# Small DMAs on the sync engine's queue, four gemm banks for two more units, and three reorderings in a two-block fp32 kernel

## Chip, cores and metric

One core of a Trainium2 chip (8 cores; the others are unused). The metric is the device time of one execution of the whole program in microseconds, as the median of several runs.

## What is computed

A token matrix x (512 tokens, width 1024, fp32) goes through two blocks. The first block, cut to what matters:

```python
h = rmsnorm(x, norm1_g); u = h @ w_in
y_a = short_conv_mixer(u_a); y_b = stick_breaking_attention(q_b, k_b, v_b)
y_c = mamba2_mixer(u_c);     y_d = moba_attention(q_d, k_d, v_d)      # 4 heads of 64 each
merged = sum(sigmoid(u_g[i]) * (y[i] @ w_branch[i]))                  # 4 branches
x = x + merged @ w_o
g, up = split(rmsnorm(x, norm2_g) @ w_gate_up)                        # hidden width 2816
x = rmsnorm(x + (silu(g) * up) @ w_down, final_g)
```

The second block takes that x. Its attention has 16 query heads and 2 key/value heads of 64, a window of three chunks of 64 keys for each chunk of 64 queries, a sink logit for each head, and a rotation of the first 16 of 64 features:

```python
h = rmsnorm(x, norm_g); q, k, v, za, u, vs, zs, gm = split(h @ w_in2)
q, k = partial_rope(q), partial_rope(k)
a  = (window_sink_attention(q, k, v, sinks) * silu(za)) @ w_att_out
sg = (chunked_spatial_gating(gelu(u), gelu(vs)) * silu(zs)) @ w_sg_out
ga, gs = split(sigmoid(gm + b_merge))
out = rmsnorm(x + (ga * a + gs * sg) @ w_o2, final_g_2)
```

## The kernel before

**Products.** Every large product is fp32 made of three passes in fp32r: a weight is split into a high part `whi` (rounded by ACT, `split`, L947) and a low part `wlo` (the difference, GpSimd, `rest`, L446), an activation into `hh` and `hl` in the same way, and TensorE sums hi*hi, lo*hi and hi*lo (`gemm_fm`, L497: L519, L520, L527). Activations lie feature-major: a tile is 128 features by 512 tokens, one PSUM bank. Weights come in units of 1024 x 256 (`raw`, `whi` and `wlo` have two slots each); a unit gives two tiles, in the branch stage four. Tile numbers T run through the whole program (`tiles_before`, L321). TensorE counts a finished tile in `tile_done`, DVE counts an evicted one in `tile_free`; before tile T TensorE waits for `free_before(T)` evictions.

**Order of the units.** Units 0 to 11 are the projections of the first block, 12 to 27 the gates and branches, 28 to 31 w_o, 32 to 65 the feed-forward in three parts (the last part ends with a down projection of 6 products in depth), 66 the second block's keys and values (tiles 164, 165), 67 to 74 its queries and za in turn (q0, za0, q1, za1, ...; tiles 166 to 181), 75 to 78 vs, then gates with w_att_out, u with zs, gates with w_sg_out, and w_o2. The bank of a tile is T mod 4, except from unit 67 (`n_qz`) to the first gate unit, where it is T mod 2, because banks 2 and 3 (`gemm23`) then hold the attention's odd steps:

```python
def bank_of(T):                                            # L325
    return G[T % 2] if tiles_before(n_qz) <= T < tiles_before(n_ga + 1) else G[T % 4]
def free_before(T):                                        # L329
    return T - 1 if tiles_before(n_qz) <= T < tiles_before(n_ga + 2) else T - 3
```

**SP (L345)** issues every load in order. It waits for the unit's slot (`slot_free`, L356: GpSimd has made the low part of the unit before last), then issues. `stream` (L372) and `stream_pairs` (L415) do that in hardware loops, L383 and L424.

**Small steps between the tiles.** The first block's heads are handled in steps that a table puts behind tiles (`MIX`, L471, `run_mix`): slot 24 + 2i + j is after tile j of branch unit 12 + i. moba's scores (`mo1`, L643) for heads 0 to 3 are in slots 25, 27, 29, 31, stick-breaking's (`st1`, L685) in 34, 37, 40, 43. TensorE works in two row halves there: `array_halves` (L292) takes one half of the rows from q and k and the other from `qs`, `ks`, copies with the two 64-partition halves exchanged. These copies are four DMAs of 256 KB, issued by ACT in slots 24 and 33 (`st_swap`, L1081 to L1091), in order with ACT's other work.

**Residual and norm.** In the w_o stage (DVE L1667, ACT L1141) and in the last down projection (DVE L1708, ACT L1167) each tile m goes round: DVE adds the residual into xT (L1665); ACT makes one (`sq0`) or two squares (`sq1`, `sq2`, L1174, L1175) and then rounds hh (L1150, L1176); DVE forms hl (L1670, L1711) and adds the squares into sums (`accumulate`, L1661). The first tile of the next unit needs hh and hl of all eight m. From the sums ACT and DVE then make the norm's factors, R with them (L1724).

**Into the second block.** DVE evicts the keys (L1734 to L1740: `rope_s` and four 64-row pieces of `k2`), then the values (`wpt`, L1742), scales all of xT by the final gain and factor (L1744 to L1746, eight operations), reads the transposed factors (L1748) and the transposed gating weights (L1751), and adds the rotated part to the keys (`finish_keys`, L1760). The rotation wants `rope_s` with rows 0 to 7 and 8 to 15 of each half exchanged, in `rope_t`; ACT issues these copies (`swap_halves`, L1232): eight for the keys, four for each pair of query tiles. DVE adds `rope_t` to a query pair (L1840) just before it evicts the za tile behind it.

**Attention.** 32 steps s, four for each tile m of two heads. Each engine has a `w_slot` that handles several steps at once, in this order:

```python
# TensorE, L859             # ACT, L1220              # DVE, L1806
w_values(i - 4)             w_out(i - 4)              w_soft(i);  w_norm(i - 1)
w_turn(i - 3)               w_turned(i - 3)           w_rest(i - 5)
w_scores(i)                 w_exp(i)                  w_out(i - 4)
```

TensorE's `w_scores(s)` (L816) waits for `w_p`, the normalised weights of step s - 2, whose bank it takes. `w_turn` transposes the weights, ACT's `w_turned` (L1203) copies them to `wpt`, `w_values` (L846) multiplies by v. Every fourth step DVE's `w_out` (L1794) makes `att_t` and ACT's `w_out` (L1214) rounds it. TensorE's slots stand in the middle and between its gemm tiles (`hook`), from tile 170 on.

Of the kernel before, what the change touches and what calls it, by code (L numbers as in the profile page):

```python
# [28 lines left out]
P = 128  # L29
# [46 lines left out]
def build_program(nc, x, par, cst1, cst2a, w_in, w_branch, w_o, w_gu, w_down, w_in2, sg_w, sg_b, ln_g,  # L76
# [8 lines left out]
    with ctx:  # L85
# [239 lines left out]
        def bank_of(T):  # L325

            return G[T % 2] if tiles_before(n_qz) <= T < tiles_before(n_ga + 1) else G[T % 4]

        def free_before(T):  # L329

            return T - 1 if tiles_before(n_qz) <= T < tiles_before(n_ga + 2) else T - 3
# [13 lines left out]
        def _(sp):  # L345
# [46 lines left out]
            for q, br in enumerate(ORDER):  # L392
                stream(n_b0 + 4 * q, 4, both(tiles_of(w_in, IN_G + br * DM), tiles_of(w_branch[br], 0, 0, 2, raw_b)))
# [32 lines left out]
            stream_pairs(n_qz, (w_in2, I2_Q), (w_in2, I2_ZA))  # L426
            stream(n_vs, 4, both(tiles_of(w_in2, I2_VS)))
# [54 lines left out]

        for st, at in enumerate((24, 33)):
            MIX.setdefault(at, []).append(("swap", st))
# [9 lines left out]
        def _(pe):  # L494
# [219 lines left out]
            def st_st3(h):  # L714
                pe.wait_ge(sem("st_w"), h + 1)
                if h >= 1:
# [5 lines left out]
                      "st3": st_st3, "swap": lambda st: None}  # L722
# [93 lines left out]
            def w_scores(s):  # L816
# [3 lines left out]
                if s == 0:  # L820
                    pe.wait_ge(sem("k_ready"), 1)
                if s >= 2:
                    pe.wait_ge(sem("w_p"), s - 1)
# [35 lines left out]
            def w_slot(limit):  # L859
                i = pos[0]  # L860
                if i >= limit and limit < STEPS:
                    return
                if 0 <= i - 4 < STEPS:
# [3 lines left out]
                if i < STEPS:  # L867
                    w_scores(i)
# [75 lines left out]
        def _(act):  # L944
# [136 lines left out]
            def st_swap(st):  # L1081

                if st == 0:
                    act.wait_ge(sem("yc_lo"), 2)
                    act.wait_ge(sem("tile_free"), tiles_before(8))
                else:
                    act.wait_ge(sem("mo_s"), HEADS)
                    act.wait_ge(sem("tile_free"), tiles_before(11))
                for half, whole in ((qs, (qd, qb)[st]), (ks, (kd, kb)[st])):
                    for to in (0, 64):  # L1090
                        act.dma_start(half[to:to + 64, :, :], whole[64 - to:P - to, :, :]).then_inc(sem("swapped"), 16)  # L1091

            none = lambda *a: None
            stages = {"dt": none, "dtT": st_dtT, "xsT": none, "acs": none, "cb": st_cb, "mh1": st_mh1, "mh2": none, "mn": st_mn,
                      "mo1": st_mo1, "mo2": st_mo2, "mo3": st_mo3, "st1": st_st1, "st2": st_st2, "st3": st_st3, "swap": st_swap}
# [45 lines left out]
            for p in range(4):  # L1141
                for j in range(2):
# [857 lines left out]
```

## Time and profile before

| | us |
|---|---|
| three runs | 1403.67, 1404.04, 1406.64 (median 1404.04) |
| the profiled execution's own time | 1403.01 |
| its span, first to last instruction | 1401.2 |
| TensorE busy | 1356.1 (97%) |
| DVE, GpSimd, ACT busy | 614.2, 593.1, 512.1 |
| mean granted TensorE clock | 0.991 |

The page's table of slices shows TensorE busy in nine tenths or more of nearly every slice; the exceptions are the first slice and two at 840 to 880 us, where the granted clock is lower too. Engines wait in queues of their own, so idle time of an engine other than TensorE says little by itself. The DMA engines are busy 30% of the time.

### The profile page before, as it was taken

The numbers are of one execution on the slowest core, as the hardware profiler recorded it, in microseconds if no ns is written. First come the engines' busy times: TensorE is split into PE (matmuls) and PEld (weight loads), VectorE is DVE, ScalarE is ACT, GpSimd is POOL, SyncE is SP. The second block draws the span as 40 slices with busy tenths as digits, with TensorE's granted clock in tenths as the row PEclk, the third lists the DMA queues.
The fourth block names the chain that finished last, engine by engine and source line by source line (L and its number), as shares of the span: only waits on it lengthen the run. The fifth ranks groups of instructions, "written<-read, shape, count | busy, mean of one in ns | idle before, by whom it ended". The sixth has DMA issues, their size and how long they took to land.

```text
span 1401.2 us, 17740 instructions
## 1 busy us (share of the span) xinstructions
PE 1356.1 (97%) x6782; PEld 1104.8 (79%) x6782; DVE 614.2 (44%) x1043; ACT 512.1 (37%) x741; POOL 593.1 (42%) x448
## 2 busy tenths in 40 slices
PE   7999999999999999999999996999999999999997
PEld 5888877788888888888888875777778888888885
DVE  3575444465544343223412356466564432333343
ACT  5222444545433443122212244244454322533232
POOL 4453333333454365444445542433322444535441
PEclk9999999999999999999999997999999999999999
DMA  6231342313224342233333223222211222232221
GB/s 197 72 109 61 90 128 76 105 38 113 76 68 151 90 120 90 90 91 107 102 90 90 75 75 108 65 94 66 64 61 61 89 91 91 74 107 90 90 91 60
DMA packets 144560, 126.41 MB, mean 90 GB/s; under 512 B 4272, under 2 KB 142640, under 8 KB 144496
## 3 DMA queue, kind: packets, MB, share of 16 engines
q1 hardware_dynamic: 143472, 122.77, 28.5%
q10 hardware_dynamic: 1024, 2.75, 0.9%
q8 instruction: 45, 0.74, 0.2%
q14 instruction: 19, 0.16, 0.0%
HBM read 120.66 MB, written 2.10 MB: 88 GB/s over the span
## 4 chain that ended last, share of the span: by engine, by line
issue 43%; POOL 28%; PE 26%; DVE 1%; ACT 1%; POOLq 0%; DVEq 0%; ACTq 0%
POOL wlo L455 27%; PE gemm L519 7%; PE gemm L520 7%; PE gemm L527 7%; PE gemm L541 1%; PE gemm L542 1%; PE gemm L543 1%; POOL wlo_b L451 1%; PE mix L854 1%; PE mix L842 1%; PE mix L911 1%; DVE sml L1876 0%; DVE wp L1790 0%; PE gemm L831 0%; PE mix L831 0%
## 5 line engine op out<-in xcount | busy, mean ns | idle before, releaser
L455 POOL TENSOR_TENSOR wlo<-raw,whi 128x512 fp32r<-128x512 f32 x428 | 572.9, 1371 | 625.6 <-ACT whi L959 625.6
L519 PE MATMUL gemm<-hh,whi 128*128 128x512 f32 x1168 | 466.6, 400 | 13.5 <-DVE hl L1711 4.8
L520 PE MATMUL gemm<-hl,whi 128*128 128x512 f32 x1168 | 458.7, 393 | 0.0
L527 PE MATMUL gemm<-hh,wlo 128*128 128x512 f32 x1168 | 290.4, 391 | 0.0
L959 ACT ACTIVATE whi<-raw 128x2048 fp32r<-128x2048 f32 x107 | 204.3, 1910 | 217.6 <-PE gemm L527 188.2
L519 PEld LDWEIGHTS gemm<-hh,whi 128*128 128x128 f32 x1168 | 221.6, 190 | 71.3 <-issue 11.5
L520 PEld LDWEIGHTS gemm<-hl,whi 128*128 128x128 f32 x1168 | 221.8, 190 | 45.1 <-issue 0.7
L527 PEld LDWEIGHTS gemm<-hh,wlo 128*128 128x128 f32 x1168 | 220.4, 189 | 46.5
L451 POOL TENSOR_TENSOR wlo_b<-raw_b,whi_b 128x512 fp32r<-128x512 f32 x16 | 20.7, 1293 | 156.1 <-ACT whi L959 156.1
L519 PE MATMUL gemm<-ah,whi 128*128 128x512 f32 x176 | 68.8, 391 | 3.2 <-DVE al L1693 3.2
L520 PE MATMUL gemm<-al,whi 128*128 128x512 f32 x176 | 68.5, 389 | 0.0
L1686 DVE TENSOR_TENSOR fu_t<-gemm,R 128x512 f32<-128x512 f32 x22 | 15.2, 692 | 102.9 <-PE gemm L527 102.9
L541 PE MATMUL gemm<-whi,hh 128*128 128x256 f32 x192 | 56.6, 295 | 0.6 <-POOL wlo L455 0.6
L542 PE MATMUL gemm<-whi,hl 128*128 128x256 f32 x192 | 54.2, 282 | 0.0
L543 PE MATMUL gemm<-wlo,hh 128*128 128x256 f32 x192 | 54.2, 282 | 0.0
L1633 DVE TENSOR_TENSOR gt<-gemm,R 128x512 f32<-128x512 f32 x32 | 22.0, 689 | 59.0 <-PE gemm L527 58.9
L976 ACT ACTIVATE gt<-gt 128x512 f32<-128x512 f32 x32 | 20.2, 631 | 73.4 <-DVE gt L1633 73.4
L1161 ACT ACTIVATE fg_t<-fg_t 128x512 f32<-128x512 f32 x22 | 13.9, 633 | 83.2 <-DVE fg_t L1684 83.2
L527 PE MATMUL gemm<-ah,wlo 128*128 128x512 f32 x176 | 43.9, 390 | 0.0
L1705 DVE TENSOR_TENSOR xT<-xT,gemm 128x512 f32 x16 | 11.0, 688 | 72.1 <-PE gemm L527 72.1
L519 PEld LDWEIGHTS gemm<-ah,whi 128*128 128x128 f32 x176 | 33.0, 188 | 11.2 <-DVE al L1693 4.5
L541 PEld LDWEIGHTS gemm<-whi,hh 128*128 128x128 f32 x192 | 36.6, 191 | 5.1 <-issue 5.0
(364 smaller groups left out, 1837.0 us busy)
## 6 DMA issues: line engine op xcount, KB each, us to landing
raw<-w_in SPq DMA_DIRECT2D x56, 1024.0 KB, 5.3
raw<-w_gu SPq DMA_DIRECT2D x44, 512.0 KB, 4.8
raw<-w_o SPq DMA_DIRECT2D x8, 1024.0 KB, 5.2
raw<-w_down SPq DMA_DIRECT2D x16, 512.0 KB, 4.0
raw_b<-w_branch SPq DMA_DIRECT2D x16, 256.0 KB, 5.6
raw<-w_ao SPq DMA_DIRECT2D x4, 1024.0 KB, 5.1
raw<-w_so SPq DMA_DIRECT2D x4, 1024.0 KB, 5.2
raw<-w_down SPq DMA_DIRECT2D x8, 384.0 KB, 3.3
```

The lines of the kernel that those rows point to most:

```text
L451: nc.gpsimd.tensor_tensor(a(wlo_b), a(raw_b), as_f32(a(whi_b)), ALU.subtract)
L455: last = nc.gpsimd.tensor_tensor(a(wlo), a(raw), as_f32(a(whi)), ALU.subtract)
L519: mm(bank[:, :], w, xh[:, k, :], start=(k == 0), stop=False)
L520: mm(bank[:, :], w, xl[:, k, :], start=False, stop=False)
L527: last = mm(bank[:, :], wlo_[:, s, k, col:col + P], xh[:, k, :], start=False, stop=(k == kts - 1))
L541: mm(o, hh[:, k, tok], whi[:, s, k, w], start=(k == 0), stop=False)
L542: mm(o, hl[:, k, tok], whi[:, s, k, w], start=False, stop=False)
L543: last = mm(o, hh[:, k, tok], wlo[:, s, k, w], start=False, stop=(k == KD - 1))
L959: fn(a(whi), a(raw), ACT.Copy).then_inc(sem("hi_done"), 1)
L976: return fn(dst, src, ACT.Tanh, scale=scale)
L1633: tt(g, G[T % 4][:, :], R[:, :], ALU.mult).then_inc(sem("tile_free"), 1)
L1686: tt(fu_t[:, s, :], G[(T + 1) % 4][:, :], R[:, :], ALU.mult).then_inc(sem("tile_free"), 1)
```

## The change

Four `dma_start` groups move from ACT's stream to SP's; two limits in `bank_of` and `free_before` move from unit 67 to unit 69, with one more wait on TensorE; the order inside the attention slot changes on TensorE and ACT; eight xT scalings of DVE move from before the factor read to the za tiles; ACT rounds before it squares in two stages. SP's loops for the first eight branch units, for the q/za pairs and for vs are written out.

```diff
         def bank_of(T):
-            return G[T % 2] if tiles_before(n_qz) <= T < tiles_before(n_ga + 1) else G[T % 4]
+            return G[T % 2] if tiles_before(n_qz + 2) <= T < tiles_before(n_ga + 1) else G[T % 4]
         def free_before(T):
-            return T - 1 if tiles_before(n_qz) <= T < tiles_before(n_ga + 2) else T - 3
+            return T - 1 if tiles_before(n_qz + 2) <= T < tiles_before(n_ga + 2) else T - 3
# SP
-            for q, br in enumerate(ORDER):
+            def swap_rows(q, k):
+                for half, whole in ((qs, q), (ks, k)):
+                    for to in (0, 64):
+                        sp.dma_start(half[to:to + 64, :, :], whole[64 - to:P - to, :, :]).then_inc(sem("swapped"), 16)
+
+            for q, br in enumerate(ORDER[:2]):
+                for u in range(4):
+                    n = n_b0 + 4 * q + u
+                    slot_free(n)
+                    load(n, cols(w_in, IN_G + br * DM + u * UC, UC))
+                    load(n, cols(w_branch[br], u * UC, UC, 0, 2), raw_b[:, n % 2])
+                    if n == n_b0 + 1:
+                        sp.wait_ge(sem("yc_lo"), 2)
+                        sp.wait_ge(sem("tile_free"), tiles_before(8))
+                        swap_rows(qd, kd)
+                    if n == n_b0 + 5:
+                        sp.wait_ge(sem("mo_s"), HEADS)
+                        sp.wait_ge(sem("tile_free"), tiles_before(11))
+                        swap_rows(qb, kb)
+            for q, br in enumerate(ORDER[2:], 2):
                 stream(n_b0 + 4 * q, 4, both(tiles_of(w_in, IN_G + br * DM), tiles_of(w_branch[br], 0, 0, 2, raw_b)))
...
-            stream_pairs(n_qz, (w_in2, I2_Q), (w_in2, I2_ZA))
-            stream(n_vs, 4, both(tiles_of(w_in2, I2_VS)))
+            def swap_rotary(p):
+                sp.wait_ge(sem("tile_free"), tiles_before(n_qz + 2 * p) + 2)
+                for r in (0, 64):
+                    for a, b in ((0, 8), (8, 0)):
+                        sp.dma_start(rope_t[r + a:r + a + 8, :, :], rope_s[r + b:r + b + 8, :, :]).then_inc(sem("rope_in"), 16)
+            for p in range(4):
+                for j, c0 in enumerate((I2_Q, I2_ZA)):
+                    n = n_qz + 2 * p + j
+                    slot_free(n)
+                    load(n, cols(w_in2, c0 + p * UC, UC))
+                    if p == 0 and j == 1:
+                        sp.wait_ge(sem("tile_free"), tiles_before(n_e0) + 1)
+                        for r in (0, 64):
+                            for a, b in ((0, 8), (8, 0)):
+                                for kv in range(2):
+                                    sp.dma_start(rope_t[r + a:r + a + 8, kv, :], rope_s[64 * kv + b:64 * kv + b + 8, 0, :])\
+                                        .then_inc(sem("rope_in"), 16)
+                    if p >= 1 and j == 0:
+                        sp.wait_ge(sem("k_ready"), 1)
+                        swap_rotary(p - 1)
+            slot_free(n_vs)
+            load(n_vs, cols(w_in2, I2_VS, UC))
+            swap_rotary(3)
+            for u in range(1, 4):
+                slot_free(n_vs + u)
+                load(n_vs + u, cols(w_in2, I2_VS + u * UC, UC))
# TensorE, w_scores
                 if s == 0:
                     pe.wait_ge(sem("k_ready"), 1)
+                if s == 1:
+                    pe.wait_ge(sem("tile_free"), tiles_before(n_qz + 2))
# TensorE, w_slot
+                if i < STEPS:
+                    w_scores(i)
                 if 0 <= i - 4 < STEPS:
                     w_values(i - 4)
                 if 0 <= i - 3 < STEPS:
                     w_turn(i - 3)
-                if i < STEPS:
-                    w_scores(i)
# ACT, w_o stage, and in the same way in the last down projection (hh ahead of sq1, sq2)
+                    fn(hh[:, m, :], xT[:, m, :], ACT.Copy, scale=pcol("g2", m)).then_inc(sem("h2_hi"), 1)
                     fn(sq0[:, m % 2, :], xT[:, m, :], ACT.Square).then_inc(sem("sq0"), 1)
-                    fn(hh[:, m, :], xT[:, m, :], ACT.Copy, scale=pcol("g2", m)).then_inc(sem("h2_hi"), 1)
# ACT, w_slot (st_swap and swap_halves are removed with their calls)
-                if 0 <= i - 4 < STEPS:
-                    w_out(i - 4)
                 if 0 <= i - 3 < STEPS:
                     w_turned(i - 3)
                 if i < STEPS:
                     w_exp(i)
+                if 0 <= i - 4 < STEPS:
+                    w_out(i - 4)
# DVE, before the factor read
-            for m in range(KD):
-                last = stt(out=xT[:, m, :], in0=xT[:, m, :], scalar=pcol("fg", m), in1=r1[:, :], op0=ALU.mult, op1=ALU.mult)
-            link(last)
# DVE, behind each q and za tile
+                        if u == 1:
+                            stt(out=xT[:, m, :], in0=xT[:, m, :], scalar=pcol("fg", m), in1=r1[:, :], op0=ALU.mult, op1=ALU.mult)\
+                                .then_inc(sem("x_scaled"), 1)
+            dve.wait_ge(sem("x_scaled"), KD)
```

## Rows read from the trace of the kernel before

**Rows 1.** The page, busy time of the engines.
```profile
PE 1356.1 (97%) x6782; PEld 1104.8 (79%) x6782; DVE 614.2 (44%) x1043; ACT 512.1 (37%) x741; POOL 593.1 (42%) x448
```

**Rows 2.** Who waited for whom, TensorE: us in total, times, longest us.
```profile
PE mix L854 <- ACT wpt L1209: 6.1, 6, 1.1
PE gemm L519 <- DVE hl L1711: 4.8, 1, 4.8
PE gemm L519 <- DVE k L1738: 3.8, 1, 3.8
...
PE mix L695 <- DMA ks<-kb: 2.3, 1, 2.3
```

**Rows 3.** Windows, three stretches behind TensorE's waits; PEclk is the granted clock.
```profile
core 0: us, PE busy (x) PEld busy (x) DVE busy (x) ACT busy (x) POOL busy (x), PEclk, DMA share, GB/s
...
267.50:272.10 4.60, 4.57 (x15) 3.28 (x16) 0.00 (x0) 2.74 (x6) 3.37 (x3) 0.63 0.05 6
...
854.70:860.50 5.80, 5.76 (x14) 4.12 (x15) 2.10 (x3) 2.29 (x2) 4.72 (x4) 0.61 0.04 11
...
870.40:876.20 5.80, 5.80 (x14) 4.54 (x15) 5.80 (x9) 0.00 (x0) 0.00 (x0) 0.50 0.09 17
```

**Rows 4.** Timeline, around the second half-swap: start us, us, engine, line, operation [idle before].
```profile
241.37 0.59 PE L654 MATMUL mix<-kd,qd 64*128 64x256 f32 x2
...
256.43 0.37 SPq L383 DMA_DIRECT2D raw<-w_in  x1
...
259.45 2.17 ACTq L1091 DMA_DIRECT2D ks<-kb  x2
...
267.53 0.66 PE L695 MATMUL mix<-qb,kb 64*128 64x512 f32 x1 [2.30 <-DMA ks<-kb]
```

**Rows 5.** Timeline, the last down projection: DVE, then ACT, then GpSimd.
```profile
814.22 0.69 DVE L1665 TENSOR_TENSOR xT<-xT,gemm 128x512 f32<-128x512 f32 x1 [2.21 <-PE gemm L527]
...
818.31 0.69 DVE L1665 TENSOR_TENSOR xT<-xT,gemm 128x512 f32<-128x512 f32 x1
...
844.85 0.68 DVE L1665 TENSOR_TENSOR xT<-xT,gemm 128x512 f32<-128x512 f32 x1
847.45 1.67 DVE L1711 SCALAR_TENSOR_TENSOR hl<-xT,sml,hh 128x512 fp32r<-128x512 f32 x1 [1.93 <-ACT hh L1176]
849.05 2.37 DVE L1661 TENSOR_TENSOR acc<-acc,sq 128x512 f32<-128x512 f32 x2
...
853.93 0.75 DVE L1711 SCALAR_TENSOR_TENSOR hl<-xT,sml,hh 128x512 fp32r<-128x512 f32 x1 [1.92 <-ACT hh L1176]
...
846.71 0.71 ACT L1176 ACTIVATE hh<-xT,sml 128x512 fp32r<-128x512 f32 x1
...
844.82 5.45 POOL L455 TENSOR_TENSOR wlo<-raw,whi 128x512 fp32r<-128x512 f32 x4 [5.51 <-ACT whi L959]
```

**Rows 6.** Timeline from tile 165 to tile 170; last, the page's median to landing.
```profile
860.52 0.79 PE L519 MATMUL gemm<-hh,whi 128*128 128x512 f32 x1
...
867.55 2.79 DVE L1738 SCALAR_TENSOR_TENSOR k<-gemm,cs 64x512 f32<-64x512 f32 x4
...
870.37 5.90 ACTq L1241 DMA_DIRECT2D rope_t<-rope_s  x8
...
888.25 0.50 PE L519 MATMUL gemm<-hh,whi 128*128 128x512 f32 x1 [2.11 <-DVE rope_q L1847]
...
893.80 1.23 DVE L1840 TENSOR_TENSOR q<-rope_q,rope_t 128x1024 f32<-128x1024 f32 x1 [4.41 <-DMA rope_t<-rope_s]
...
899.27 0.39 PE L519 MATMUL gemm<-hh,whi 128*128 128x512 f32 x1
...
raw<-w_in SPq DMA_DIRECT2D x56, 1024.0 KB, 5.3
```

**Rows 7.** Timeline of one attention slot (TensorE, DVE, ACT); last, DVE's waits for odd scores.
```profile
1028.13 0.44 PE L854 MATMUL mix<-wpt,v 128*64 128x128 f32 x4 [0.98 <-ACT wpt L1209]
...
1025.23 1.12 DVE L1790 TENSOR_TENSOR wp<-mix,sml 64x384 f32<-64x384 f32 x2
...
1027.12 0.63 ACT L1218 ACTIVATE ath<-att_t 128x512 fp32r<-128x512 f32 x1 [5.35 <-DVE att_t L1798]
...
DVE gemm L1777 <- PE gemm L831: 24.7, 13, 2.5
```

More of the change, by code:

```diff
@@ L481, in build_program @@
                         MIX.setdefault(at, []).append(step)
-        for st, at in enumerate((24, 33)):
-            MIX.setdefault(at, []).append(("swap", st))
         def run_mix(stages, slot):
@@ L721, in _ @@
                       "mn": st_mn, "mo1": st_mo1, "mo2": st_mo2, "mo3": st_mo3, "st1": st_st1, "st2": st_st2,
-                      "st3": st_st3, "swap": lambda st: None}
+                      "st3": st_st3}
             for n in range(N_A):
@@ L1079, in st_st3 @@
                 out_hi(M[3], "st_o", yh[0], "yb_hi", h)
[L1081 to L1091, printed above, removed]
             none = lambda *a: None
             stages = {"dt": none, "dtT": st_dtT, "xsT": none, "acs": none, "cb": st_cb, "mh1": st_mh1, "mh2": none, "mn": st_mn,
-                      "mo1": st_mo1, "mo2": st_mo2, "mo3": st_mo3, "st1": st_st1, "st2": st_st2, "st3": st_st3, "swap": st_swap}
+                      "mo1": st_mo1, "mo2": st_mo2, "mo3": st_mo3, "st1": st_st1, "st2": st_st2, "st3": st_st3}
             def st_mh2(h):
@@ L1173, in _ @@
                         act.wait_ge(sem("acc2"), m - 1)
+                    fn(hh[:, m, :], xT[:, m, :], ACT.Copy, scale=fgng[:, m:m + 1]).then_inc(sem("h3_hi"), 1)
                     fn(sq1[:, m % 2, :], xT[:, m, :], ACT.Square)
                     fn(sq2[:, m % 2, :], xT[:, m, :], ACT.Square, scale=pcol("fg", m)).then_inc(sem("sq12"), 1)
-                    fn(hh[:, m, :], xT[:, m, :], ACT.Copy, scale=fgng[:, m:m + 1]).then_inc(sem("h3_hi"), 1)
             split(n_e0 + 1)
@@ L1229, in w_slot @@
                     w_exp(i)
+                if 0 <= i - 4 < STEPS:
+                    w_out(i - 4)
                 pos[0] += 1
-            def swap_halves(tiles, T):
-                act.wait_ge(sem("tile_free"), T)
-                for r in (0, 64):
-                    for a, b in ((0, 8), (8, 0)):
-                        if tiles == 2:
-                            act.dma_start(rope_t[r + a:r + a + 8, :, :], rope_s[r + b:r + b + 8, :, :]).then_inc(sem("rope_in"), 16)
-                        else:
-                            for kv in range(2):
-                                act.dma_start(rope_t[r + a:r + a + 8, kv, :], rope_s[64 * kv + b:64 * kv + b + 8, 0, :])\
-                                    .then_inc(sem("rope_in"), 16)
             def attention_gate(m):
@@ L1249, in attention_gate @@
                 sigmoid(za_e[:, m % 2, :], za_tile(m)).then_inc(sem("za_e"), 1)
-            swap_halves(1, tiles_before(n_e0) + 1)
             for p in range(4):
@@ L1256, in _ @@
                     for j in range(2):
-                        if u == 1 and j == 0:
-                            swap_halves(2, tiles_before(n) + 2)
                         w_slot(lim)
@@ L1588, in _ @@
             stages = {"dt": st_dt, "dtT": st_dtT, "xsT": st_xsT, "acs": st_acs, "cb": st_cb, "mh1": st_mh1, "mh2": st_mh2, "mn": st_mn,
-                      "mo1": st_mo1, "mo2": none, "mo3": st_mo3, "st1": st_st1, "st2": st_st2, "st3": st_st3, "swap": none}
+                      "mo1": st_mo1, "mo2": none, "mo3": st_mo3, "st1": st_st1, "st2": st_st2, "st3": st_st3}
             for n in range(N_A):
```

## The prediction

> **What bounds the kernel now.** TensorE does: the page gives it 1356.1 us busy in a span of 1401.2 [rows 1], so nothing is gained by making another engine idle; only TensorE's own waits and its slow stretches can go. The list of who waited for whom names them [rows 2]: 6.1 us in six waits for the attention's transposed weights (wpt), 4.8 for the last low half of h3 (hl), 3.8 for the keys' eviction, 2.3 for the second half-swap (ks from kb), and the timeline adds 2.11 for an evicted rotary tile [rows 6]. The table of stretches adds what follows such a wait: the granted clock is 0.63 in the 4.6 us after the swap's wait, 0.61 in the 5.8 us after the hl wait, 0.50 in the 5.8 us after the keys' wait [rows 3]. A stretch at 0.50 does half the work, so these cost 0.37 x 4.6 = 1.7, 0.39 x 5.8 = 2.3 and 0.50 x 5.8 = 2.9 us of work. Everything outside runs at 1.00 with TensorE busy, so a microsecond saved here should reach the end.
>
> **Half-swaps moved to SP (lines 1081 to 1091).** The last mo scores, which free qs and ks and give mo_s its fourth count, end at 242.0; ACT issues the second swap's last two copies only at 259.45, for 2.17 us, and TensorE, ready at 265.2, waits until 267.5 [rows 4], 5.9 us after the last issue. The new order lets SP issue at 242, its load for unit 17 being out by then. Four issues of about 1 us end at 246, and with the same 5.9 us the data is there at 252, 13 us before it is wanted. That removes 2.3 us of waiting and the 1.7 us of slow clock behind it: **4.0 us**; at least 2.3 if the clock falls for another reason. SP's next load now stands behind these copies, but it goes out only when GpSimd frees the slot, at 256.43 in the old trace, so nothing is late. The first swap was waited for by nobody and stays so.
>
> **Rounding ahead of the squares (lines 1149, 1174 to 1176).** In the last down projection each of the eight tiles goes round: DVE adds the residual, ACT squares twice and rounds hh, DVE forms hl, then adds two squares. DVE waits 1.93 us for hh in every turn [rows 5]. The residuals begin at 814.22 and 818.31, TensorE's pace of 4.1 us a tile, but the last begins at 851.3, where the sums from 849.05 end: 37.1 us for seven turns, so it is the DVE chain that is late. A turn beside a GpSimd pass takes 851.3 - 844.85 = 6.5 us (hl 1.67, sums 2.37); three such, one at TensorE's pace and three calm ones (hl 0.75) of 4.5 are 37.1. With hh first DVE waits for its 0.71 us alone instead of 1.93, but the sums still wait for both squares (about 2.0). A calm turn becomes 0.65 + 2.0 + 1.25 = 3.9, so TensorE's 4.1 holds. A shared turn becomes 0.65 + 0.75 + 1.6 + 2.4 = 5.4 if its sums cost as now, or 6.2 if, being earlier, all three DVE operations fall beside GpSimd. From the first residual: two turns at 4.1, then 5.4, 3.9, 5.4, 3.9, 5.4 (the late ones at DVE's pace) is 32.2 against 37.1, plus 1.2 for the last hl: 6.1 us earlier. With 6.2 for the three it is 3.9 earlier. I take 5.0, the middle.
> The hl row of 1.67 us beside GpSimd's 5.45 us pass, against 0.75 alone, is the row that speaks against this edit. The Trainium skill (SBUF — State Buffer, section "SBUF: two separate sides") says that a DVE operation with two SBUF inputs and a GpSimd operation lock each other out of a shared port pair for a whole instruction; by that rule hl and both sums would always wait once each in a shared turn, which is the 3.9.
> TensorE goes on when the last hl is there; it was idle 4.8 us before. The clock loss of 2.3 us may stay or shrink; the 2.1 us wait that ended at 888.25 was followed by no drop, as the unit behind it keeps 11.0 us for two tiles, one of 2.3 by 0.63 [rows 3, 6]. I count 0.6 of it. Together **5.6 us**, between 3.9 and 8.4 (6.1 + 2.3). The same edit in the w_o stage gives nothing: no wait on sq0 or h2 is in the list.
>
> **Four banks longer (bank_of, free_before), the residual scaling taken out of the chain.** Let K be the start of the k/v unit's second tile (165), 860.52; unit q0's tiles are 166 and 167, za0's 168 and 169. From K to tile 168 at 888.25 is 27.7 us [rows 6]. In it lie 3.8 (tile 166 waited for tile 164's eviction, only because both banks of the pair were in use), 2.9 of slow clock and 2.1 (tile 168 waited for 166's). With T - 3 neither wait binds: 18.9 us of work is left. **8.8 us** gone; 5.9 if the clock falls all the same.
> Next late is the eviction of tile 168, which DVE makes after the queries' rotation, and tile 170 needs its bank. Tile 164's keys are out at 870.34, K + 9.8; SP then issues eight copies, at ACT's price 5.9 us: K + 15.7. The four query copies took 4.4 us from eviction to landing in all; less four issues of 0.74 the landing is 1.5, and the keys are there at K + 17.2. k2's addition 1.2 ends before v2 can go (it needs tile 167's turn, K + 18.9); v2 0.7, two rotary evictions of two operations, 0.7 each: K + 22.4. Four copies 4.4: K + 26.8, q2 1.2, tile 168's eviction 0.7: K + 28.7. TensorE wants its bank after two more tiles (899.27 - 888.25 = 11.0): K + 29.9. So 1.2 us to spare and no wait. The eight xT scalings, operations of the residual's size and so about 0.7 us each, sat between wpt and these evictions. Spread over the za tiles they lie in DVE's idle time and cost nothing: it waited 24.7 us, 13 times, for the odd steps' scores alone [rows 7]. If that cover were gone, each would delay an eviction by 0.7.
> SP holds the load of each za unit until the query tiles before it are evicted and four copies issued (2.9 us); it lands 5.3 us after its issue [rows 6]. Unit za1's is wanted at K + 42.8 and lands at K + 22.4 + 2.9 + 5.3 = K + 30.6, before ACT reaches it after score 0.
>
> **Scores first, ACT's w_out last.** Each wait of the 6.1 us has one pattern [rows 7]: at every fourth step ACT stands in w_out until DVE has att_t (ath from 1027.12), copies wpt only behind it, and TensorE's values wait 0.98 until 1028.13. With wpt and the exponentials ahead of w_out that wait has no cause: **6.1 us**, 5.0 if a part comes back. A slot has the same products as before.
>
> **Sum.** 4.0 + 5.6 + 8.8 + 6.1 = 24.5 us off the profiled execution's 1403.0 (span 1401.2) gives 1378.5. The median of the three runs, 1404.0, is 1.0 above that execution; from it the sum gives **1379.5**. All low bounds (2.3 + 3.9 + 5.9 + 5.0 = 17.1) give 1387, all high ones (4.0 + 8.4 + 8.8 + 6.1 = 27.3) 1377.
>
> **Rivals.**
> (a) The chain of small copies becomes the bound. If SP needs more for an issue than ACT's 0.74 us (5.90 for eight), twelve issues in the chain use up the 1.2 us at 0.1 us each. At 1.0 us an issue, the price of the half-swap's copies (2.17 for two), it is up to 4 us late: about 3 us of idle and 2.9 of clock come back at tile 170, so 1385.4. For it: those copies stand in one row, and SP also waits for k_ready ahead of the query ones. Against: SP's own load was issued in 0.37 us [rows 4]. Chance 0.13.
> (b) DVE now paces the attention: the waits go, but others of that size replace them (its eight scalings are new there). The 6.1 is lost: 1385.6. Against: its waits for scores average 24.7 / 13 = 1.9 us [rows 7]. Chance 0.12.
> (c) The swap doesn't come earlier, because SP reaches it late: 4.0 lost, 1383.5. Chance 0.03.
> (d) Slower: scores stand first in the slot and wait for w_p of two steps before, where values and turn (about 1 us) used to cover them; all behind them on TensorE is held. With the DVE step (wp) ending at 1026.35 and the slot beginning at 1027.15, before its 0.98 of wait [rows 7], 0.8 us is spare even in the old order, and scores now start the DVE step 1 us earlier. It decides against the change from (24.5 - 6.1) / 32 = 0.6 us of wait a step; at 1.2 us a step it is 38 us lost: 1404 + 38 - 18.4 = 1424. Chance 0.04.
> My forecast keeps 0.68.
>
> **Chances and range.** About 0.2% (2.8 us) is what a measurement of this kernel can tell from no change. The forecast and (a) to (c) hold 0.96 and are all faster; 0.01 of it I leave for several of them together, which ends near no change. So faster 0.95, same 0.01, slower 0.04 from (d). The range takes the forecast's bounds and (a) to (c), with 3 to 4 us on either side, because two of the rivals can come together and the clock may do better than I count: 1372 to 1390.
>
> **What would show it.** Right: no wait on ks from kb and clock 1.00 there; hh about 0.7 us after each residual and TensorE's hl wait under 4 us; tiles 166 and 168 without a wait, the distance K to tile 168 at 19 us; no 1 us wait for wpt in the attention. Wrong: a wait before tile 170 with rope_t as its root (a), about 1 us waits of scores for w_p (b, d), a late raw transfer before a za unit. If the K distance stays above 25 us, the bank step fails.

## The result and the profile after

The changed kernel takes **1373.2 us** (median of four runs, 1371.7 to 1375.0) against 1403.9 for the kernel before on the same chip: ratio 0.978, 95% interval 0.976 to 0.979. That is 30.6 us faster, where 24.5 were forecast. The profiled execution took 1375.0 with a span of 1373.2, so it lies 1.8 above the median. Times here and below are medians of the fast executions; one execution of `round_back`, 2503.9 us at a mean clock of 0.81, is in no median.

First the page's engine row (it answers to [rows 1]) and TensorE's part of the list of who waited for whom (to [rows 2]).

```profile
PE 1345.7 (98%) x6782; PEld 1101.9 (80%) x6782; DVE 617.2 (45%) x1043; ACT 511.4 (37%) x741; POOL 597.5 (44%) x448
```

```profile
PE gemm L604 <- DMA xtm<-x: 9.0, 1, 9.0
PE gemm L561 <- DVE hl L1728: 3.5, 1, 3.5
PE gemm L561 <- DVE al L1710: 3.2, 3, 1.7
```

The waits for wpt, for the keys, for rope_q and for ks are gone, hl is down from 4.8 to 3.5. One more wait of the kernel before is gone, which neither the rows nor the prediction had: the start of tile 164. From its list, and from its timeline:

```profile
PE gemm L519 <- issue: 2.1, 1, 2.1
```

```profile
844.84 0.47 PE L519 MATMUL gemm<-hh,whi 128*128 128x512 f32 x1 [2.09 <-issue]
```

That product needs the high part of unit 66's weights, and ScalarE split it from 842.85 to 844.74, behind its squares and rounding. Between 844.8 and 849.9 the granted clock was then 0.67, where the prediction had "everything outside runs at 1.00". (The page's slices of before have one slice below nine tenths busy between the first and the last, 841 to 876 us, and it alone has the lower clock.) In the changed kernel the split starts at 838.31, tile 164 starts at 840.86 without a wait, and the clock is 1.00 from 838 to 844.2.

The span shrank by 28.0 us, but these waits and the ones in the timeline explain only part of it: TensorE is also *busy* 10.4 us less, with the same 6782 products. Part of that is the slow clock, and part, as the experiments show, is something that the prediction had not seen.

The windows: first an early stretch that ran at 1.00 in the trace of before, then those behind the old waits (to [rows 3]).

```profile
core 0: us, PE busy (x) PEld busy (x) DVE busy (x) ACT busy (x) POOL busy (x), PEclk, DMA share, GB/s
104.00:112.00 8.00, 8.00 (x38) 6.84 (x38) 1.75 (x4) 0.00 (x0) 0.60 (x1) 0.79 0.44 133
267.30:271.90 4.60, 4.60 (x23) 3.53 (x23) 1.74 (x2) 4.33 (x8) 3.12 (x3) 1.00 0.09 13
846.00:848.00 2.00, 0.29 (x1) 0.29 (x2) 0.87 (x2) 1.85 (x3) 0.65 (x1) 0.63 0.90 266
848.00:852.00 4.00, 4.00 (x10) 3.17 (x10) 2.20 (x3) 3.20 (x3) 1.40 (x2) 0.50 0.76 257
852.00:854.00 2.00, 2.00 (x4) 0.92 (x4) 0.00 (x0) 0.00 (x0) 2.00 (x2) 0.66 0.00 0
```

Behind the half-swap the clock now stays at 1.00; behind the hl wait it still falls.

Then the timeline: SyncE's copies for the second half-swap and TensorE's use of them (to [rows 4]), the last down projection on VectorE and ScalarE (to [rows 5]), and tile 165 to tile 170 (to [rows 6]).

```profile
243.54 0.59 PE L696 MATMUL mix<-kd,qd 64*128 64x256 f32 x2
...
244.17 1.11 SPq L395 DMA_DIRECT2D qs<-qb  x2
245.31 1.65 SPq L395 DMA_DIRECT2D ks<-kb  x2
...
267.32 0.69 PE L737 MATMUL mix<-qb,kb 64*128 64x512 f32 x1
...
812.49 0.69 DVE L1682 TENSOR_TENSOR xT<-xT,gemm 128x512 f32<-128x512 f32 x1 [2.21 <-PE gemm L569]
...
839.65 0.68 DVE L1682 TENSOR_TENSOR xT<-xT,gemm 128x512 f32<-128x512 f32 x1
841.12 1.02 DVE L1728 SCALAR_TENSOR_TENSOR hl<-xT,sml,hh 128x512 fp32r<-128x512 f32 x1 [0.79 <-ACT hh L1206]
842.25 3.27 DVE L1678 TENSOR_TENSOR acc<-acc,sq 128x512 f32<-128x512 f32 x2
845.44 0.67 DVE L1682 TENSOR_TENSOR xT<-xT,gemm 128x512 f32<-128x512 f32 x1
...
847.71 0.80 PE L561 MATMUL gemm<-hh,whi 128*128 128x512 f32 x1 [3.52 <-DVE hl L1728]
...
854.06 0.80 PE L561 MATMUL gemm<-hh,whi 128*128 128x512 f32 x1
...
872.57 0.48 PE L561 MATMUL gemm<-hh,whi 128*128 128x512 f32 x1
...
876.13 2.64 SPq L450 DMA_DIRECT2D rope_t<-rope_s  x4
...
880.55 1.83 DVE L1854 TENSOR_TENSOR q<-rope_q,rope_t 128x1024 f32<-128x1024 f32 x1 [4.49 <-DMA rope_t<-rope_s]
882.41 0.69 DVE L1383 SCALAR_TENSOR_TENSOR za<-gemm,R 128x512 f32<-128x512 f32 x1
...
883.56 0.39 PE L561 MATMUL gemm<-hh,whi 128*128 128x512 f32 x1
```

K (tile 165) is 854.06 here, tile 168 starts at 872.57 (K + 18.5) and tile 170 at 883.56 (K + 29.5), without a wait. Its bank came free at 883.1, less than half a microsecond ahead.

To see where the 28.0 us of span went, cut both traces at the same five instructions of TensorE: the last kd,qd scores group (240.40 before, 242.58 after), the first st_h product (284.26, 282.54), tile 165 (860.52, 854.06), the first attention scores (902.08, 886.38) and the first product of the gated output (1084.84, 1056.82). Such cuts carry no noise from outside their stretch, and every experiment below is read with them:

| stretch | before | after | gain | forecast |
|---|---|---|---|---|
| start to the kd,qd scores | 240.40 | 242.58 | -2.2 | 0 |
| kd,qd scores to st_h | 43.86 | 39.96 | 3.9 | 4.0 |
| st_h to tile 165 | 576.26 | 571.52 | 4.7 | 5.6 |
| tile 165 to scores 0 | 41.56 | 32.32 | 9.2 | 8.8 |
| attention: scores 0 to gated output | 182.76 | 170.44 | **12.3** | **6.1** |
| the rest | 316.36 | 316.38 | 0.0 | 0 |

The first line is no effect of an edit: the first product came 0.3 us later (9.03 against 8.73), the group of 20 small products at 103 us 0.6 later, and the window from 104 to 112 ran at a mean clock of 0.79 in this execution. Of the four runs the two with a mean clock of 0.997 took 2.2 to 3.3 us less than the two with 0.993 and 0.995. Three terms are where they were forecast; the attention gained twice its term. The experiments asked what the second six microseconds are, and whether the other terms have the causes given to them.

### The profile page after: what moved, and what is told of

It is laid out like the page before. It is cut to its first block, busy times and chain, and to the rows that moved or that the text cites. A ratio compares the mean times of both kernels' runs of the same rounds, so it can differ in the third digit from the quotient of the medians.

```text
span 1373.2 us, 17654 instructions
## 1 busy us (share of the span) xinstructions
PE 1345.7 (98%) x6782; PEld 1101.9 (80%) x6782; DVE 617.2 (45%) x1043; ACT 511.4 (37%) x741; POOL 597.5 (44%) x448
## 3 DMA queue, kind: packets, MB, share of 16 engines
q1 hardware_dynamic: 144496, 125.52, 29.9%
## 4 chain that ended last, share of the span: by engine, by line
issue 42%; POOL 28%; PE 27%; DVE 1%; ACT 0%; POOLq 0%; DVEq 0%
POOL wlo L500 28%; PE gemm L561 7%; PE gemm L562 7%; PE gemm L569 7%; PE gemm L583 1%; PE gemm L584 1%; PE gemm L585 1%; POOL wlo_b L496 1%; PE mix L898 1%; PE mix L886 1%; PE mix L955 1%; DVE sml L1894 0%; PE gemm L875 0%; PE mix L875 0%; POOLq L505 0%
## 5 line engine op out<-in xcount | busy, mean ns | idle before, releaser
L569 PEld LDWEIGHTS gemm<-ah,wlo 128*128 128x128 f32 x176 | 33.0, 188 | 6.9
```

Of the source, the lines that this page charges most:

```text
L569: last = mm(bank[:, :], wlo_[:, s, k, col:col + P], xh[:, k, :], start=False, stop=(k == kts - 1))
```

## The experiments

All kernels start from the changed one. "Stretch" means a line of the table above.

**Where the attention's 12.3 us come from.** The slot has three groups of small fp32 products: scores of step i, values of i-4, turn (transposes) of i-3. Four kernels reorder them, one engine at a time. `pe_last`:

```diff
+                if 0 <= i - 4 < STEPS:
+                    w_values(i - 4)
+                if 0 <= i - 3 < STEPS:
+                    w_turn(i - 3)
                 if i < STEPS:
                     w_scores(i)
-                if 0 <= i - 4 < STEPS:
-                    w_values(i - 4)
-                if 0 <= i - 3 < STEPS:
-                    w_turn(i - 3)
```

> The changed kernel (1373.2 us) with TensorE's order in an attention slot put back: values, turn, scores; ScalarE keeps the new order. Theory A (who stands behind the turns): of the 12.3 us that the attention stretch gained, 6.1 are the six waits for the turned weights, and the rest is the turn of 4 transposes, which takes 0.59 us to the next instruction with scores behind it and 0.41 with a projection behind it; by it this kernel is 31 x 0.18 = 5.5 us slower (1378.7), L886 stands 0.59 before the scores again, and no wait for wpt returns, because ScalarE no longer does the output's step ahead of the weights. Theory B (all of it is early scores): the exponentials and the softmax start later, the waits come back too, 10 to 12 us slower (1383 to 1385). Theory C (the order on TensorE is neutral, as the prediction had it): 1373, within 1.5.

Measured: 1379.4 us; attention stretch 176.74, 6.3 longer; no wait for wpt, only 0.4 us in two waits for att_t.

`pe_mid` (values, scores, turn):

> The changed kernel with values, scores, turn on TensorE: the scores 0.6 us later in the slot, but no scores behind the transposes. Theory A: as the changed kernel within 0.5 us (1373), turns 0.41 to the next instruction. Theory B (early scores): part of the gain goes, 2 to 6 us slower (1375 to 1379).

Measured: 1374.3 us; attention stretch 171.07, 0.6 longer, of which 0.5 is a longer wait for wlo (0.9 against 0.4). So the scores need not be first.

`pe_stv` (scores, turn, values):

> The changed kernel with scores, turn, values on TensorE. It tells what it is behind the transposes that costs. Theory A1 (any small fp32 product behind the transposes, since its weights are fp32 too): 32 turns take 0.59 again, 5.5 us slower (1378.7). Theory A2 (only the scores, whose products use a 64 x 64 part of the array): turns stay near 0.41, within 1 us of the changed kernel. Theory B expects no loss either, since the scores are still first; the length of L886 to the next instruction in the trace tells A2 from B only together with the other runs.

Measured: 1379.3 us; attention stretch 175.46, 5.0 longer, no waits.

`act_first` puts ScalarE's w_out(i - 4) back ahead of w_turned and w_exp, and leaves TensorE alone:

> The changed kernel with ScalarE's order put back (the output's step w_out, then the turned weights, then the exponential); TensorE keeps scores first. Theory A: the six waits of about 1 us of the values for wpt are made by this order alone, since w_out stands behind the chain of small vector steps at each group's last step: 5 to 6 us slower (1379), six waits for wpt in the list, turns at 0.41. Rival (TensorE's order took the waits away, ScalarE's is neutral): 1373 within 1.5 and no such waits.

Measured: 1376.8 us; attention stretch 171.98, 1.5 longer. The list has 0.2 us of waiting for wpt and 1.6 for wlo (0.4 in the changed kernel), and no 1 us waits. Theory A's 5 to 6 us were wrong for this kernel. The median is high for such a stretch: its profiled execution took 1373.6 and the other three 1376.7 to 1377.0, at the lower mean clock.

The turns are read in TensorE's timeline. Each line is a group with its start; the next line's start less its own is what the group cost. First the kernel before, a slot with scores behind the turn and, from the end of the attention, one where no scores are left:

```profile
1022.57 0.66 PE L854 MATMUL mix<-wpt,v 128*64 128x128 f32 x8
1023.17 0.44 PE L842 MATMUL mix<-c,wp 128*128 128x128 f32 x2
1023.53 0.56 PE L831 MATMUL gemm<-k,q 64*64 64x192 f32 x8
1024.02 0.39 PE L541 MATMUL gemm<-whi,hh 128*128 128x256 f32 x1
...
1067.32 0.66 PE L842 MATMUL mix<-c,wp 128*128 128x128 f32 x4
1067.73 0.36 PE L541 MATMUL gemm<-whi,hh 128*128 128x256 f32 x1
```

The changed kernel, then `pe_last`, then `pe_stv`:

```profile
1007.95 0.56 PE L875 MATMUL gemm<-k,q 64*64 64x192 f32 x8
1008.43 0.66 PE L898 MATMUL mix<-wpt,v 128*64 128x128 f32 x8
1009.03 0.65 PE L886 MATMUL mix<-c,wp 128*128 128x128 f32 x4
1009.44 0.36 PE L583 MATMUL gemm<-whi,hh 128*128 128x256 f32 x1
```

```profile
1012.46 0.66 PE L886 MATMUL mix<-c,wp 128*128 128x128 f32 x4
1013.05 0.56 PE L875 MATMUL gemm<-k,q 64*64 64x192 f32 x8
```

```profile
1011.21 0.66 PE L886 MATMUL mix<-c,wp 128*128 128x128 f32 x4
1011.80 0.66 PE L898 MATMUL mix<-wpt,v 128*64 128x128 f32 x8
```

A turn of four transposes takes 0.41 us to the next instruction when a projection follows (1009.03 to 1009.44) and 0.59 when another small fp32 product does, scores (`pe_last`) or values (`pe_stv`). Two transposes take 0.36 (before, 1023.17 to 1023.53) against 0.19 in the changed kernel. So it is 0.17 to 0.18 us once a slot, whatever the number of transposes. Eight scores cost 0.48 to 0.49 and eight values 0.59 to 0.60, whatever stands beside them. Twenty-nine slots have scores behind a turn in the old order: 29 x 0.18 = 5.2 us; added up over the stretch, the turns take 16.4 us in the kernel before and 11.4 in the changed one, which is 5.0. One other distance changes with the order: the first projection product behind a slot takes 0.34 us to the next (0.22 where it is 256 wide) behind scores, and 0.31 (0.20) behind transposes; over the stretch that is 0.6 us, in `pe_last` as in the kernel before. The trace of before had it already, in the slot at 1067.32, which has no scores and needs 0.41. Theory A1 stands (any small fp32 product, not only the 64 x 64 ones).

**What took the waits away.** Neither order alone brings them back, so both were put back together:

> The changed kernel with the old order of the attention slot on both engines: values, turn, scores on TensorE and w_out, turned weights, exponential on ScalarE; all other parts stay changed. Either order alone left no wait for wpt, so the question is what took the six waits away. Theory D (either order is enough): with both back the waits are back too, attention stretch 182.8 us as before, 12.3 slower than the changed kernel: about 1385.5. Theory E (the waits went with another part: ScalarE's copies, the banks or the scaling): only the 5.5 us behind the transposes, 1378.7, and no waits for wpt in the list.

Measured: 1387.8 us; attention stretch 183.19, 12.8 longer. From TensorE's waits of `both_last`:

```profile
PE mix L898 <- ACT wpt L1241: 6.1, 6, 1.1
```

The same six waits as before [rows 2]. So theory D: either engine's order is enough to remove them. The account of the 12.3: 6.1 of waits, 5.0 behind the transposes, 0.6 at the first projection product behind the slot and 0.2 of a shorter wait for wlo are 11.9. The 0.4 left is in nothing that was measured.

**Banks** (`banks_back`: G[T % 2] and T - 1 from tiles_before(n_qz) on, the wait of scores 1 taken out):

> The changed kernel with two banks of gemm from the first query unit on, as before, and without the extra wait of the second scores; the copies stay on SyncE. Theory F (banks alone, as the prediction had it): from the start of tile 165 to tile 168 it is 27.7 us again against 18.5, 9 us slower, 1382. Rival G (part of the old 27.7 was the copies' issuing on ScalarE, 5.9 us between the evictions): the stretch takes 21 to 25 us, 1376 to 1380.

Measured: 1382.6 us; tile 165 to scores 0 takes 41.84, 9.5 longer, the other stretches as in the changed kernel. TensorE's waits of this kernel:

```profile
PE gemm L561 <- DVE k L1753: 3.8, 1, 3.8
...
PE gemm L561 <- DVE rope_q L1859: 2.1, 1, 2.1
```

Theory F: both old waits return to the digit, with SyncE still issuing the copies. The distance named for it did not: K to tile 168 is 26.4 us, not 27.7, and the rest of the 9.5 lies behind tile 168. The clock explains both. In the kernel before it fell behind the first wait alone (0.50 for 5.8 us, 2.9 of work [rows 3]) and was 1.00 behind the second; here it was 0.52 from 863.7 to 867.0 and 0.55 from 880.2 to 884.0, 1.6 and 1.7 us, 3.3 of the 3.6 beside the waits.

**Rounding ahead of the squares** (`round_back`: the hh line behind the squares again, in both stages):

> The changed kernel with the squares ahead of the rounding again, in both places. By the prediction's step, as the traces have it: the last product of tile 164 stands 5.3 us later and the slow clock behind it costs 0 to 1 us more: 1378.5 to 1379.5; the wait for hl 4.8 instead of 3.5. Rival (the chain behind it, from the sums to the keys, is the bound at tile 170, so that the 5.3 are partly there already): 1375 to 1377.

Measured: 1380.0 us; st_h to tile 165 takes 576.17, 4.7 longer, the hl wait is 4.8, the wait of 2.1 at tile 164's start and the low clock behind it (0.66 from 843.4 to 848.4) are back, all other stretches are as in the changed kernel. The rival falls: nothing of the gain was covered. The edit in the w_o stage gives nothing, as forecast: the first residual of the last down projection comes 529.9 to 530.0 us after the first st_h product with either order.

**Half-swaps** (`halves_act`: the swap steps on ScalarE's list at slots 24 and 33 again):

> The changed kernel with the two swaps of the rows' halves issued by ScalarE again. By the prediction: wait of 2.3 us for ks by kb at 267 us and 1.7 us of the slow clock behind it, 4.0 slower: 1377.2, mean granted clock lower there (0.63 between 267 and 272). Rival (the clock's part was not bound to this wait): 1375.5.

Measured: 1379.3 us by the median of four, but the profiled execution took 1375.0. Its stretch around the swap is 43.45, 3.5 longer than in the changed kernel. TensorE's timeline at the wait, then the window behind it:

```profile
266.99 0.66 PE L732 MATMUL mix<-qb,kb 64*128 64x512 f32 x1 [1.90 <-DMA ks<-kb]
```

```profile
267.00:271.60 4.60, 4.60 (x15) 3.39 (x16) 0.43 (x1) 2.92 (x6) 4.03 (x3) 0.64 0.02 4
```

1.9 of waiting and 0.36 x 4.6 = 1.7 of clock make 3.6, so the clock's part does hang on this wait. The other runs took 1379.0 to 1379.7, at a mean clock of 0.992 against 0.995 in the profiled one; compared with the changed kernel's runs of lower clock (1374.3 and 1375.0) that is 4.7 more, and where the 1.2 above the stretch's 3.5 comes from is open, since they have no trace. The medians alone, 6.0 apart, would overstate the edit.

**The residual scaling** (`scale_back`: all eight ahead of the copy of rcol again):

> The changed kernel with VectorE's eight scalings of the residual ahead of the copy of the transposed rows again. Theory H (they stand on the chain that reaches tile 170): 8 x 0.85 = 6.8 us from 864.6, of which 3.7 reach the sum of the keys at 870.94; the changed kernel has 0.5 to spare before tile 170, so TensorE waits 3.2 there and the time is 1376.4. Rival I (the chain of copies hides them): 1373.2, the stretch from tile 165 to the first scores 32.3 as before this edit. Rival J (they cost their full length): 1379.

Measured: 1377.9 us; tile 165 to scores 0 takes 35.05, 2.7 longer; TensorE waits 2.3 us at tile 170 for za. Theory H, at 2.7 instead of 3.2: the scalings took 7.45 us, and k2's addition came 4.3 later against K (875.94 with K at 854.75, where the changed kernel has 870.94 and 854.06). Of that 3.6 reaches the queries' sum, because v2, behind the addition, waits 0.7 for TensorE in the changed kernel. The attention stretch is 170.00, 0.4 shorter than in the changed kernel, whose 0.4 us wait for wlo is not in this list.

**The rotary copies** (`rotary_act`: swap_halves on ScalarE again):

> The changed kernel with the small copies of the keys' and queries' rotary halves issued by ScalarE again, all else changed. Theory K (they cost nothing either way once the banks are four and ScalarE's attention order is new): 1373 within 1, tile 165 to first scores 32.3, attention stretch 170.4. Theory L (they were a part of the gain: each pair of query tiles holds ScalarE for 2.6 us inside a slot, and the exponential and turned weights behind it come late): attention stretch 171.5 to 174, 1374.5 to 1377, with waits for wpt or w_p in the list.

Measured: 1377.8 us. Neither K nor L: the attention stretch is 170.45, untouched, but tile 165 to scores 0 takes 36.91, 4.6 longer, of which 2.7 is a wait for za at tile 170 and the rest the clock (0.63 between 884 and 888). The cause is in the timeline of `rotary_act` (ScalarE's queue, SyncE's queue, whose one line covers two issues, and VectorE):

```profile
873.02 2.65 ACTq L1244 DMA_DIRECT2D rope_t<-rope_s  x4
...
874.40 9.72 SPq L443 DMA_DIRECT2D raw<-w_in  x2
...
880.52 2.08 DVE L1843 TENSOR_TENSOR q<-rope_q,rope_t 128x1024 f32<-128x1024 f32 x1 [7.53 <-DMA rope_t<-rope_s]
```

The copies are issued at the same distance from K as in the changed kernel (K + 22.0) and as fast (2.65 against 2.64), but they are there 7.5 us after the first issue instead of 4.4. SyncE, which no longer has to issue them, sends out a 1 MB load in between. The windows from 876 to 880, of `rotary_act` and then of the changed kernel; the last two numbers are the DMA share and GB/s:

```profile
876.00:880.00 4.00, 4.00 (x19) 3.34 (x18) 0.00 (x0) 1.69 (x1) 2.24 (x2) 1.00 0.87 262
```

```profile
876.00:880.00 4.00, 4.00 (x20) 3.30 (x19) 0.06 (x1) 1.44 (x1) 2.49 (x2) 1.00 0.24 34
```

`rotary_hold` tests that: ScalarE still issues the copies, and SyncE waits with the load.

```diff
                     slot_free(n)
+                    if p >= 1 and j == 1:
+                        sp.wait_ge(sem("rope_in"), 128 + 64 * p)
                     load(n, cols(w_in2, c0 + p * UC, UC))
```

> The kernel with the small rotary copies on ScalarE, and one thing more: SyncE issues the 1 MB load of the next unit but one only once the query pair's copies have landed. In the kernel without that, the copies were issued at 873.02 (2.65 us) and VectorE waited for them until 880.52, 7.5 us, with the load issued at 874.40 and 262 GB/s moving between 876 and 880; with SyncE issuing both in turn it was 4.4 us. Theory P (the copies came late because the load moved beside them): 4.4 to 4.6 us from the first copy's issue to the query's sum, no wait at tile 170, tile 165 to the first scores 32.3, 1373. Rival Q (ScalarE's queue is slower for such copies, load or not): 7 us or more again, tile 165 to the first scores 36.9, 1377.8.

Measured: 1373.3 us; tile 165 to scores 0 takes 32.30, and the timeline has:

```profile
873.55 2.65 ACTq L1250 DMA_DIRECT2D rope_t<-rope_s  x4
...
877.93 1.23 DVE L1849 TENSOR_TENSOR q<-rope_q,rope_t 128x1024 f32<-128x1024 f32 x1 [4.41 <-DMA rope_t<-rope_s]
```

Theory P is shown: which engine issues the copies is worth nothing, that the load stays behind them is worth 4.4 us by the medians and 4.6 in the stretch. The Trainium skill (DMA: Bandwidth & Descriptors, section "Queues, rings and completion order") says that each of the 16 DMA engines takes turns, a packet at a time, between the queues that have work for it, SyncE's and ScalarE's among them. By that rule a small copy on one queue shares the engines with a large load on the other, and the rows above agree: 3.1 us longer beside 262 GB/s.

**A version that beats both.** What is left is the hl wait and its clock. `fill_gate` fills it with work that needs no new data, and takes the bank of tile 168 out of the queries' chain:

```diff
-            gemm_fm(T, n_e0, n_e0 % 2, hh, hl, KD, 0, True, ready=("h3_lo", 0))
+            high(0, range(KD - 1))
+            pe.wait_ge(sem("tile_free"), free_before(T + 1))
+            high(1, range(KD - 1))
+            high(0, (KD - 1,))
+            low(0)
...
-            gemm_fm(T + 1, n_e0, n_e0 % 2, hh, hl, KD, P, False)
+            high(1, (KD - 1,))
+            low(1)
...
                         if u == 1 and j == 0:
+                            if p == 0:
+                                scaled(T, za_tile(m), 0.5)
                             dve.wait_ge(sem("rope_in"), 128 + 64 * (p + 1))
...
-                            scaled(T, za_tile(m), 0.5)
+                            if m:
+                                scaled(T, za_tile(m), 0.5)
```

(high(j, ks) is the loop of the products with whi for tile T + j and those k, low(j) the eight with wlo.)

> A version meant to beat both. The changed kernel still waits 3.5 us for the last low part of the third norm's input ahead of tile 164's last products, and runs at the low clock behind it (0.50 to 0.66 between 846 and 854). Here tile 165's products of the first seven row blocks (14 x 0.23 = 3.2 us) stand ahead of tile 164's last row block, and VectorE evicts tile 168 ahead of the sum of the first query pair, which waits 4.5 us for its copies. Theory M (nothing else binds within 6 us: the chain of copies starts 2.6 us earlier, and the gate's bank no longer hangs on it): 3.2 of the wait and 2.9 of the slow clock go, 1367. Rival N (the chain to the first scores is the bound, 0.5 to spare there): 2.6 to 3.1 us, 1370. Rival O (the products that fill the wait delay the chain itself): 1373.

Measured: **1369.6 us** (1367.4 to 1370.0), ratio to the kernel before 0.9745, interval 0.973 to 0.976, where the changed kernel has 0.9777. From st_h to scores 0 it takes 597.99 against 603.84: 5.8 us. TensorE's wait for hl is down to 0.4:

```profile
PE gemm L832 <- DVE hl L1750: 0.4, 1, 0.4
```

and the windows (columns as above) have the full clock where the changed kernel had 0.50 to 0.66:

```profile
846.00:848.00 2.00, 1.68 (x8) 1.07 (x6) 1.20 (x2) 1.52 (x3) 1.00 (x1) 1.00 1.04 359
848.00:852.00 4.00, 3.96 (x15) 2.74 (x15) 2.21 (x3) 2.46 (x3) 0.15 (x1) 1.00 0.87 283
852.00:854.00 2.00, 2.00 (x9) 1.50 (x8) 0.00 (x0) 1.96 (x3) 2.00 (x2) 1.00 0.01 3
```

How much of it is the edits' is less sure than the 5.8. The changed kernel's trace has the lower of two clock levels behind the hl wait; six experiments with the same code there have the higher one (below) and take 602.5 to 602.7 us from st_h to scores 0 where nothing else was changed in that stretch, so the gain is 4.5 to 5.9. The medians differ by 3.6 and were not taken beside each other; by them alone it would be rival N, whose time of 1370 was met. The stretch and the list speak against N, since no wait before the first scores took the place of the old one. So it lies between N and M, nearer M, and the medians' shortfall stays open. The two edits in it were not tried apart.

## Why the prediction was right, and where its size was off

**Half-swaps, 4.0.** Measured 3.9 in the stretch, 3.5 when undone. SyncE issued at 244.17, at once behind the last mo scores (243.54 and 0.59), as forecast; the 2.2 us against 242 are the late start of this trace. Its four copies took 2.8 us instead of four; that changes nothing, since the data is wanted at 267.3. Rival (c) is out.

**Rounding, 5.6.** The middle of the range was taken for the turns, and it was right, by luck as much as by working, since no row decided between its ends: residuals follow each other by 4.09, 4.08, 5.56, 3.81, 5.81, 3.81 and 5.79 us, where 4.1, 4.1 and then 5.4 to 6.2 beside 3.9 were forecast. hl beside GpSimd takes 1.02 instead of 1.67, but the sums 3.27 instead of 2.37 [rows 5], so the wait for GpSimd moved from one to the other. The shared turns lie between the two ends, 5.4 and 6.2. The Trainium skill (SBUF — State Buffer, section "SBUF: two separate sides") states that the one of two such operations that starts first holds the shared port pair for its whole instruction and the other waits. That sets no fixed wait: it depends on how much of the other's instruction is left. The trace agrees with such waits, hl at 0.27 over its 0.75 alone and the two sums together at 1.98 over their 1.29; that each of the three "would always wait once", the prediction's own step from the rule to 6.2, it doesn't bear out. The last hl came 5.3 earlier (5.0 forecast). TensorE's side of the 5.3, which the prediction put down to its 4.8 of idle time alone, is 1.3 of the hl wait, 2.1 of the wait at tile 164's start and about 1.8 of the low clock behind that. The 0.6 for the clock behind hl can't be told from the spread between executions: from the products that waited for hl to tile 165 it takes 5.78 us before, 6.35 in the changed kernel's trace and 5.1 to 5.3 in six of the experiments with the same code there. The stretch from st_h to tile 165 takes 571.5 to 571.8 us in the changed kernel and four of the experiments with that code, and 570.2 to 570.4 in the six, so 1.2 of it is not the edit's, and the term is 4.7 to 5.9.

**Banks, 8.8.** Measured 9.2, and 9.5 when undone: K to tile 168 is 18.5 where 18.9 stood. The spare time at tile 170 was put at 1.2 and is 0.4 to 0.5, since the chain ended at K + 29.0 instead of 28.7 and TensorE came at 29.5 instead of 29.9. Rival (a) was therefore close, but not by its cause: SyncE's issue costs 0.69, less than ScalarE's 0.74. The price in (a), 1.0 us an issue, was that of one pair; ScalarE's first half-swap in the same trace has four issues in 2.8 us. And its sum doesn't follow: twelve issues 0.26 dearer are 3.1 us, 1.9 beyond the spare time, where it has about 3 of idle. What would have used the spare time up is a load that moves beside the copies. The prediction priced SyncE's order only for what it delays; that it also protects the copies, worth 4.6 us, was not in it. The scalings at their new place cost 0.4 at most, and at the old one they would have taken 2.7 of the gain.

**Attention, 6.1.** This is the term that was mis-sized: 12.3 measured. The waits were priced rightly and went (6.1). The sentence that failed is "A slot has the same products as before": it has, but their order has a price, 0.18 us for a small fp32 product behind transposes, 29 times. The total missed by 30.6 - 24.5 = 6.1, and the attention's term by 12.3 - 6.1 = 6.2, of which 5.0 are behind the transposes and 0.6 behind the slot. The reason given for the waits was half right: ScalarE's w_out ahead of wpt is needed for them, but so is TensorE's order, and either edit alone takes them away (but for 0.2 us). Rivals (b) and (d) did not happen: scores wait for nothing in the list.

**The total.** 1373.2 is below 1377, which all the high bounds of the terms together give. It lies in the stated 1372 to 1390 only by the margin, which is 5 us on the low side, not the 3 to 4 that are named, and which was given for two rivals at once and for the clock. Neither filled it; the order of the small products did. That the time is inside the range is luck; the direction, the removed waits and three of the four terms are not.

## What to carry to other kernels

Read what an instruction costs as the distance to the next start, and compare it between all the neighbours it has in a trace: an order of small products that is neutral by their number cost 0.2 us each time round the loop here. Keep large loads from starting between the issue and the landing of small copies that a chain waits for, on whichever queue they are. And where TensorE waits for the last block of its input, products of the next tile with the blocks already there fill the wait and keep the clock up.

## What the runs showed of the hardware that was not expected

Four fp32 transposes of 128 x 128 take 0.41 us to the next product if that is one of the projections, 0.58 to 0.59 if it is an fp32 product of scores or values; two take 0.19 against 0.36. The cause is not known, only that it goes with the neighbour. The first projection product behind the group takes 0.34 us to the next behind scores and 0.31 behind transposes.

Four copies of 32 KB landed 4.4 us after their first issue where the next 1 MB load started 2.7 us or more behind it (SyncE issuing both, or ScalarE with the load held back), and 7.5 where it started 1.4 us behind it on the other queue.

Between 104 and 112 us, with TensorE busy throughout, the mean granted clock was 0.79 in some executions and 1.00 in others whose code is the same up to there (the changed kernel and `pe_last` against `act_first`); where it fell, the stretch from the group of 20 small products at 103 us to the kd,qd scores took 1.6 us more (138.9 against 137.3). With the 1.2 us ahead of tile 165 this makes 2.8 us, about the distance between the runs of one kernel. A difference of 3 us between two medians of four may be that alone.
